# Up projection of a decoder step as a one-level Strassen product

## Chip, cores and metric

One NeuronCore of a Trainium2 chip. The metric is the device time of one execution, in microseconds (us), of the only core. TensorE is called PE below, VectorE DVE, ScalarE ACT, GpSimd POOL and the queue that issues the DMAs SP.

## The reference

One layer of a decoder, for 2048 prompt tokens and 32 sample tokens (8 sequences of 4), width 1024, in float32:

```python
h = rms_norm(x) * (1 + sc1) + sh1
proj = h @ w_in                          # two groups of heads: retention and mLSTM
x = x + g1 * (concat(y_r, y_m) @ w_out)
h2 = rms_norm(x) * (1 + sc2) + sh2
u, val = split(h2 @ w_up, [2816])        # w_up is 1024 x 5632
u = causal_conv3(u)                      # depthwise, three taps
x = x + g2 * ((silu(u) * val) @ w_down)
y = rms_norm(x) * final_w
```

The last rows of u before the convolution are outputs too. The change is in `h2 @ w_up`.

## The kernel before

Float32 accuracy is had from float16 parts. Each operand is scaled by a power of two and cut in two: a high part (ACT, a cast to float16) and a low part (DVE, value less high part). `three_passes` (L267) then adds three matmuls into one float32 bank: high by high, high by low, low by high.

The phases follow each other with a barrier between them. `phase_out` (L1573) multiplies the mixed heads by `w_out`, adds the residual, norms, and leaves `h2` transposed in SBUF, cut in its two parts (`core.h2`, features on partitions, tokens along the free axis). `phase_up` (L1918) reads it. `phase_down` (L2179) does the rest.

**phase_out** runs over 16 chunks of 128 prompt tokens and one of 32. On PE a step is the product of chunk c (48 matmuls), the transposes of the normed chunk c-1 (`turn_x`) and of the input of chunk c+2 (`turn_y`). On DVE a step is, in this order: the mean of chunk c-1, the low part of y for c+1, the scale of c+2 (a reduction and six small operations), `residual` of c (waits for the product), `h_full` of c-1 (two operations over 128x1024, `modulate`, L274) and `h_lo` of c-1, which waits for ACT's `h_hi`. ACT's order in a step is `y_hi`, `norm_x`, `scale_y`, `square`, `h_hi`. POOL does only a tiny power for each chunk (`x_rms`). The weights of the first block of `w_up` are prepared near the end of this phase.

**phase_up** runs over 22 blocks of 128 of the 2816 channels, and in a block over 5 groups of 416 tokens. For a group PE does 8 x 3 = 24 matmuls for u (bank `pu`) and 24 for val (bank `pv`). ACT copies u out (L2038), makes the first tap (L2047) and the tanh (L2056). DVE adds the two other taps (L2102), makes z (L2114), multiplies by val out of PSUM (L2118) and reduces the maximum (L2120). SP stores the result. Five groups make one block.

The next block's weights (`UpWeights`, L1870) are prepared meanwhile: SP loads them, DVE finds their maximum (L1891), POOL spreads it over the partitions (L1899, `PARTITION_ALL_REDUCE`, behind a one-element `TENSOR_TENSOR`, L1898), DVE makes the power of two (L153 to L158), ACT cuts the high part (L1903) and DVE the low part (L1907). The semaphore `lo_cut` then lets PE begin the block and SP load the block after the next. DVE also reduces the maximum of a block of `w_down` (L2143).

The order of the work on each engine is written out by hand, one queue per engine, with semaphores between them. Nothing is reordered at run time.

Of the kernel before, what the change touches and what calls it, by code (L numbers as in the profile page):

```python
# [24 lines left out]
ALU = mybir.AluOpType  # L25
# [7 lines left out]
P = 128  # L33
# [15 lines left out]
PT = [min(TG, SEQ - g * TG) for g in range(NG)]  # L49
RMS_EPS, GN_EPS = 1e-6, 1e-5  # L50
# [50 lines left out]
class Core:  # L101


    def __init__(self, nc, ctx, io):
# [9 lines left out]
        self.w_gate = self.sb(ctx, "w_gate", [P, 2, KC, P], F16)  # L114
# [36 lines left out]
def power_of_two(nc, steps, big, scale, inverse, bits):  # L151
# [188 lines left out]
def phase_ada(core):  # L340
# [3 lines left out]
    with ExitStack() as ctx:  # L344
# [96 lines left out]
        def _(dve):  # L441
# [18 lines left out]
            def factors():  # L460
# [4 lines left out]
                for s in range(2):  # L465
# [7 lines left out]
                    steps.then(last)  # L473
                nc.vector.tensor_copy(red[:, 6:8], red[:, 0:2]).then_inc(bound_here, 1)
# [1098 lines left out]
def phase_out(core):  # L1573
    nc, io = core.nc, core.io
    with ExitStack() as ctx:  # L1575
        sb, ps = (lambda *a: core.sb(ctx, *a)), (lambda *a: core.ps(ctx, *a))
        w = sb("out_w", [P, 2, KC, D], F16)
        g_p, g_s = sb("g1_p", [P, D]), sb("g1_s", [NS, D])
        y, ys = sb("o_y", [P, D]), sb("o_y_scaled", [P, D])
        sc, bits = sb("o_scales", [P, 8]), sb("o_bits", [P, 1], I32)  # L1580
        yp = sb("o_y_parts", [P, 2, 2, KC, P], F16)
        x, x1, xn = sb("o_x", [P, D]), sb("o_x1", [P, D]), sb("o_xn", [P, D])
        junk, st, half = sb("o_junk", [P, D], F16), sb("o_stats", [P, 4]), sb("o_minus_half", [P, 1])
        hf, h = sb("o_h_full", [P, KC, P]), core.h2
# [3 lines left out]
            "x_turned h_full h_hi h_lo steps half").split()}  # L1588
        part = lambda c, i, T: h[:, i, :, bass.ds(c * P, T)]
        block = ctx.enter_context(nc.Block())  # L1590
        x_rows = io["x_prompt"][0].rearrange("(c p) n -> c p n", p=P)
        xs = io["x_sample"].rearrange("b s n -> (b s) n")

        @block.sync
        def _(sp):
# [3 lines left out]
            sp.dma_start(g_p[:], core.g[0, 0:1].broadcast_to([P, D])).then_inc(s["const"], 16)  # L1599
            for u in range(DS):  # L1600
                sp.dma_start(g_s[u:NS:DS, :], core.g[0, 1:NC9]).then_inc(s["const"], 16)
# [30 lines left out]
            load_x(xs, NCH, NS)  # L1632
            save_x1(NCH, NS)
# [58 lines left out]
        def _(act):  # L1692
# [21 lines left out]
            def h_hi(c, T):  # L1714
                act.wait_ge(s["h_full"], c + 1)
                nc.scalar.copy(part(c, 0, T), hf[:, :, 0:T]).then_inc(s["h_hi"], 1)
# [8 lines left out]
            def step(c, buf, Tn):  # L1725
                y_hi(c + 1, P, 1 - buf)
# [5 lines left out]
            def pair(i):  # L1732
                step(2 * i + 1, 1, P)
                step(2 * i + 2, 0, P)

            pair(0)
            with act.Fori(1, NCH // 2 - 2) as i:
                pair(i)
            step(NCH - 3, 1, P)
            step(NCH - 2, 0, NS)  # L1740
            core.up.cut_hi(act, 0, 0)
# [3 lines left out]
            h_hi(NCH - 2, P)  # L1745
            norm_x(NCH - 1, P)
            square(NCH, NS)
            h_hi(NCH - 1, P)
            norm_x(NCH, NS)
            h_hi(NCH, NS)  # L1750

        @block.vector
        def _(dve):
# [16 lines left out]
            def residual(c, T, buf, g, steps):  # L1770
# [30 lines left out]
            dve.wait_ge(s["const"], 16 * (1 + DS))  # L1801
# [609 lines left out]
```

## Time and profile before

| | |
|---|---|
| median of 3 runs | 2946.09 us (2944.9 to 2947.54) |
| profiled execution, first to last instruction | 2944.8 us |
| PE matmuls busy | 2724.9 us, 93% |
| DVE busy | 1510.0 us, 51% |
| ACT busy | 797.8 us, 27% |
| POOL busy | 182.9 us, 6% |
| mean granted clock of PE | 0.958 of 2.4 GHz |

The profile is of one execution. PE's matmuls are pipelined: a recorded duration holds the drain, so the distance between two starts is what one costs, and a busy PE need not be a fast one. Idle time of an engine names what ended it. Idle time "until issue" is time in which the engine waited for nothing that the profile shows.

### The profile page before, as it was taken

The numbers are of one execution on the slowest core, as the hardware profiler recorded it, in microseconds if no ns is written. First come the engines' busy times: TensorE is split into PE (matmuls) and PEld (weight loads), VectorE is DVE, ScalarE is ACT, GpSimd is POOL, SyncE is SP. The second block draws the span as 40 slices with busy tenths as digits, with TensorE's granted clock in tenths as the row PEclk, the third lists the DMA queues.
The fourth block names the chain that finished last, engine by engine and source line by source line (L and its number), as shares of the span: only waits on it lengthen the run. The fifth ranks groups of instructions, "written<-read, shape, count | busy, mean of one in ns | idle before, by whom it ended". The sixth has DMA issues, their size and how long they took to land. (4 is left out here: it accounts for less than half of the span.)

```text
span 2944.8 us, 43573 instructions
## 1 busy us (share of the span) xinstructions
PE 2724.9 (93%) x16908; PEld 1547.6 (53%) x16908; DVE 1510.0 (51%) x3258; ACT 797.8 (27%) x1234; POOL 182.9 (6%) x220
## 2 busy tenths in 40 slices
PE   7898879988898999599789999999999987999998
PEld 1255445556777786355345555555555543444443
DVE  3555455544677676478645555555555545212221
ACT  1222222213444444044323222222222224111110
POOL 0022222220000000000000000000000000000000
PEclk9899899998999999699899999999999998999999
DMA  9712322143020100443122121222112217233230
GB/s 323 226 56 95 94 94 85 51 145 107 26 86 22 54 32 10 132 141 126 66 56 70 55 66 59 63 63 67 60 55 69 65 42 265 85 85 101 68 87 25
DMA packets 198730, 256.14 MB, mean 87 GB/s; under 512 B 16690, under 2 KB 146018, under 8 KB 197876
## 3 DMA queue, kind: packets, MB, share of 16 engines
q1 hardware_dynamic: 198652, 255.13, 27.7%
q8 instruction: 46, 0.75, 0.1%
q14 instruction: 32, 0.25, 0.0%
HBM read 179.88 MB, written 75.21 MB: 87 GB/s over the span
## 5 line engine op out<-in xcount | busy, mean ns | idle before, releaser
L269 PE MATMUL d_po<-d_w,d_a_parts 128*128 128x512 f16 (+1 forms) x748 | 285.5, 382 | 23.3 <-DVE d_w L2330 22.6
L269 PE MATMUL pu<-h_parts,u_w 128*128 128x416 f16 x880 | 299.1, 340 | 2.1 <-PEq L1575 2.1
L270 PE MATMUL pu<-h_parts,u_w 128*128 128x416 f16 x880 | 299.0, 340 | 0.0
L271 PE MATMUL pu<-h_parts,u_w 128*128 128x416 f16 x880 | 298.9, 340 | 0.0
L269 PE MATMUL pv<-h_parts,u_w 128*128 128x416 f16 x880 | 298.3, 339 | 0.0
L270 PE MATMUL pv<-h_parts,u_w 128*128 128x416 f16 x880 | 298.3, 339 | 0.0
L271 PE MATMUL pv<-h_parts,u_w 128*128 128x416 f16 x880 | 298.3, 339 | 0.0
L270 PE MATMUL d_po<-d_w,d_a_parts 128*128 128x512 f16 (+1 forms) x748 | 285.4, 382 | 0.0
L271 PE MATMUL d_po<-d_w,d_a_parts 128*128 128x512 f16 (+1 forms) x748 | 285.1, 381 | 0.0
L2102 DVE SCALAR_TENSOR_TENSOR u_cv<-u_in,u_conv,u_cv 128x416 f32<-128x416 f32 (+1 forms) x220 | 141.6, 644 | 199.8 <-ACT u_cv L2047 112.5
L269 PE MATMUL prj<-w_heads,h_parts_t 128*128 128x512 f16 (+1 forms) x544 | 209.2, 384 | 9.9 <-DVE h_parts_t L795 5.0
L270 PE MATMUL prj<-w_heads,h_parts_t 128*128 128x512 f16 (+1 forms) x544 | 208.8, 384 | 0.0
L271 PE MATMUL prj<-w_heads,h_parts_t 128*128 128x512 f16 (+1 forms) x544 | 208.5, 383 | 0.0
L269 PE MATMUL m_prj<-m_h,w_heads 128*128 128x128 f16 (+1 forms) x1088 | 179.5, 218 | 11.6 <-DMA m_h<-h_parts 10.3
L270 PE MATMUL m_prj<-m_h,w_heads 128*128 128x128 f16 (+1 forms) x1088 | 179.5, 218 | 0.0
L271 PE MATMUL m_prj<-m_h,w_heads 128*128 128x128 f16 (+1 forms) x1088 | 179.4, 218 | 0.0
L2317 DVE SCALAR_TENSOR_TENSOR d_out<-d_po,d_scale,g_p 128x1024 f32<-128x1024 f32 x16 | 20.5, 1283 | 287.1 <-PE d_po L271 287.1
L2038 ACT ACTIVATE u_in<-pu,u_scale 128x416 f32<-128x416 f32 (+1 forms) x110 | 65.9, 600 | 375.3 <-PE pu L271 375.3
L2056 ACT ACTIVATE u_th<-u_cv 128x416 f32<-128x416 f32 x110 | 60.4, 550 | 295.5 <-DVE u_cv L2102 258.9
L2274 ACT ACTIVATE d_a_parts<-d_a,mscale 128x2816 f16<-128x2816 f32 (+1 forms) x16 | 40.5, 2532 | 348.5 <-PE d_po L271 337.6
L269 PEld LDWEIGHTS d_po<-d_w,d_a_parts 128*128 128x128 f16 (+1 forms) x748 | 73.5, 98 | 114.9 <-issue 17.9
L269 PEld LDWEIGHTS pu<-h_parts,u_w 128*128 128x128 f16 x880 | 86.2, 98 | 70.1 <-issue 2.8
(384 smaller groups left out, 4982.0 us busy)
## 6 DMA issues: line engine op xcount, KB each, us to landing
wa<-in_w_ada_dram SPq DMA_DIRECT2D x12, 2048.0 KB, 21.7
act_cols<-u_a SPq DMA_DIRECT2D x110, 208.0 KB, 1.9
u_raw<-in_w_up_dram SPq DMA_DIRECT2D x44, 512.0 KB, 5.1
d_a<-act_cols SPq DMA_DIRECT2D x15, 1408.0 KB, 7.4
win_raw<-in_w_in_dram SPq DMA_DIRECT2D x8, 2048.0 KB, 18.5
u_wd<-in_w_down_dram SPq DMA_DIRECT2D x22, 512.0 KB, 3.6
d_raw<-in_w_down_dram SPq DMA_DIRECT2D x11, 1024.0 KB, 7.0
x_t<-in_x_prompt_dram SPq DMA_DIRECT2D x16, 512.0 KB, 4.2
```

What stands on the lines that cost most here:

```text
L269: nc.tensor.matmul(out, left[0], right[0], start=(k == 0), stop=False)
L270: nc.tensor.matmul(out, left[0], right[1], start=False, stop=False)
L271: return nc.tensor.matmul(out, left[1], right[0], start=False, stop=last)
L2038: last = nc.scalar.activation(ub[:, u, 2 + t:2 + t + n], bank[:, 0:n], ACT.Copy, scale=kv[:, u, 0:1])
L2056: nc.scalar.activation(th[:, x], cv[:, x], ACT.Tanh).then_inc(s["tanh"], 1)
L2102: ins = nc.vector.scalar_tensor_tensor(out=cv[:, x, 0:n], in0=ub[:, u, t + j:t + j + n], scalar=cw[:, u, j:j + 1], in1=cv[:, x, 0:n], op0= ...
L2274: nc.scalar.activation(ap[:, buf, 0, :, 0:T], a[:, :, 0:T], ACT.Copy, scale=core.mscale[:, 0:1]).then_inc(s["a_hi"], 1)
L2317: last = nc.vector.scalar_tensor_tensor(out=out[0:T], in0=po[0:T, buf].rearrange("p q n -> p (q n)"), scalar=ks[0:T], in1=g[0:T], op0=ALU. ...
```

## The change

The product `W^T h2` of one block is seen as a 2 x 2 block product. The rows of the left side are u and val of the block's 128 channels, the contraction is halved (4 of the 8 chunks of 128 features each), and the columns are even and odd chunks of 128 tokens. A one-level Strassen product (in Winograd's form) makes it from seven products of half the contraction, in place of eight.

- Tokens go in 3 groups of 3, 3 and 2 pairs of chunks (widths 384, 384 and 256 + 16 columns for each product). A product is 4 x 3 = 12 matmuls. A block has 3 x 7 x 12 = 252 matmuls in place of 240, over 12 x 7 x (384 + 384 + 272) = 87,360 columns in place of 99,840.
- The sums of the operands: for the weights, POOL makes four sums of 128x512 for each block (`UpWeights.sums`), ACT and DVE cut them as they cut the weights themselves (`cut_hi_sums`, `cut_lo_sums`, 128x2048), beside the weights' own parts (`cut_hi_own`, `cut_lo_own`, 128x1024 and 128x512). For the tokens, POOL makes four sums of 128x512 for each pair of chunks in `phase_out` (`h_sums`), with `sums_hi` on ACT and `sums_lo` on DVE (128x2048).
- The sums of the results are made on DVE and ACT: `keep_p1` (ACT), `keep_p16`, `odd_u` (two), `even_u`, `odd_val`, each 384 columns out of PSUM. Val of the even chunks is multiplied straight out of PSUM (`even_vz`), val of the odd ones on POOL (`odd_vz`).
- The convolution and the tanh go over 768 tokens at a time.
- The weights of `w_out` and of the up blocks share one piece of SBUF (`core.wide`), and so do the y parts and the weight sums (`core.spare`): the first block's weights are cut after the last product of `phase_out`.
- The gates `g1` of the sample tokens are loaded at the end of `phase_out` into the tile of the prompt's gates.

```diff
+UPAIRS = (3, 3, 2)
# phase_out, POOL (x_rms as before, and for each pair of chunks)
+                nc.gpsimd.tensor_tensor(t(3), b(odd, 1), b(odd, 0), ALU.subtract)
+                steps.then(nc.gpsimd.tensor_tensor(t(1), b(odd, 0), b(even, 0), ALU.subtract))
+                steps.then(nc.gpsimd.tensor_tensor(t(2), b(odd, 1), t(1), ALU.subtract))
+                nc.gpsimd.tensor_tensor(t(0), b(even, 1), t(2), ALU.subtract).then_inc(s["sums"], 1)
...
             core.up.reduce(pool, 0, 0)
-            x_rms(NCH - 2, P)
             x_rms(NCH - 1, P)
             x_rms(NCH, NS)
+            pool.wait_ge(s["prod"], NCH + 1)
+            core.up.sums(pool, 0)
+            pair_sums(NPAIR - 1)
# phase_out, ACT, one step
                 square(c, P)
-                h_hi(c - 1, P)
+                if j == 0 and not first:
+                    sums_hi(n - 1)
+                h_hi(n, j)
# phase_out, DVE, one step
+                if j == 0 and not first:
+                    sums_lo(n - 1)
+                h_full(n, j, P, steps, first)
+                h_lo(n, j)
# phase_out, DVE, the end
+            core.up.find_max(dve, 0, 0)
+            step(NPAIR - 1, 0, P, NS, 0, steps)
             core.up.find_scale(dve, 0, 0, steps)
-            step(NCH - 1, P, NS, 0, 1, steps, g_p)
+            step(NPAIR - 1, 1, NS, 0, 0, steps)
...
-            core.up.cut_lo(dve, 0, 0)
+            core.up.cut_lo_own(dve, 0, 0)
+            sums_lo(NPAIR - 1)
+            h_full(NPAIR, 0, NS, steps)
+            core.up.cut_lo_sums(dve, 0, 0)
...
# phase_up, PE: one group (product = 12 matmuls)
+            def opening(it, b, u, g, first=False):
+                if g == 0:
+                    pe.wait_ge(up.lo_cut, b + 1)
...
+                product(u, g, 1, px[:, g], True).then_inc(s["p1"], 1)
...
+                product(u, g, 6, py[:, x], True).then_inc(s["p6"], 1)
...
+                    product(u, g, 5, pz[:, x], True)
+                    pe.wait_ge(s["o1_here"], it + 1)
+                    product(u, g, 2, px[:, g], False).then_inc(s["p2"], 1)
+                    pe.wait_ge(s["o2_here"], it + 1)
...
+                    product(u, g, 7, py[:, x], False).then_inc(s["p7"], 1)
+                    if g + 1 < UG:
+                        opening(it + 1, b, u, g + 1, first)
+                    elif not last:
+                        opening(it + 1, b + 1, 1 - u, 0, first)
                     if g == 1:
                         turn_state(b)
...
+                    pe.wait_ge(s["o3_here"], it + 1)
+                    product(u, g, 4, py[:, x], False).then_inc(s["p4"], 1)
+                    pe.wait_ge(s["odd_here"], it + 1)
+                    product(u, g, 3, pz[:, x], False).then_inc(s["p3"], 1)
# phase_up, ACT: one group
+                    if not (first and g == 0):
+                        tanh(it - 1, (g - 1) % UG, first and g == 1)
...
+                        keep_p1(it + 1, b, u, g + 1, first and g == 0)
...
+                    if g == 1 and not last:
+                        up.cut_hi_sums(act, b + 1, 1 - u)
...
+                    tap0(it, b, u, g, first and g == 0)
+                    if g == 0 and not last:
...
+                        up.cut_hi_own(act, b + 1, 1 - u)
# phase_up, DVE: one group
+                    if prior:
+                        even_vz(it - 1, pu, pg)
+                    if g == 0 and not last:
+                        up.find_max(dve, b + 1, 1 - u)
+                    if g == 1 and not last:
+                        up.cut_lo_own(dve, b + 1, 1 - u)
+                        state_in(b)
...
+                    odd_u(it, u, g)
+                    if prior:
...
+                        gate(it - 1, (3 * i if back >= 0 else 3 * i - 3) + (back % 6) // 2, back % 2, pg, back % 6)
...
+                    if g == 2 and not last:
+                        block_scalars(b + 1, 1 - u)
...
+                        keep_p16(it + 1, u, g + 1)
...
+                    even_u(it, u, g)
+                    odd_val(it, u, g, first and g == 0)
+                    convolve(it, u, g, steps)
+                    if g == 0 and not last:
                         up.find_scale(dve, b + 1, 1 - u, steps)
+                    if g == 1 and not last:
+                        up.cut_lo_sums(dve, b + 1, 1 - u)
+                    if g == 2:
+                        keep_last(b, u)
...
                         nc.vector.tensor_reduce(wd_max[:, bass.ds(b, 1)], wd[:], AX.X, ALU.max, apply_absolute_value=True).then_inc(s["wd_maxed"], 1)
# phase_up, POOL: one block
+                if not last:
+                    up.reduce(pool, b + 1, 1 - u)
+                    up.sums(pool, b + 1)
+                for g in range(UG):
+                    odd_vz(UG * b + g, g, first and g == 0)
```

`gate` of a group waits for `odd_vz` of it (semaphore `vz_odd`). `state_in(b)` waits for PE's `turn_state(b)`. `up.sums` waits for the loaded weights and for the cut of the block before. The scale of the weights leaves two bits of room for the sums, the bound of the activations is multiplied by 4 (one small operation in `phase_ada`), and `w_gate` has moved to another allocation. In all other phases nothing is changed.

## Rows read from the trace of the kernel before

**Rows 1.** Busy time by stretch (us, PE, PEld, DVE, ACT, POOL, PEclk, DMA): phase_out, phase_up.

```profile
1237.00:1481.70 244.70, 215.00 (x1080) 111.12 (x1080) 167.21 (x290) 90.50 (x101) 9.82 (x19) 0.93 0.34 114
1481.70:2426.10 944.40, 938.43 (x5324) 520.08 (x5324) 500.89 (x936) 258.22 (x417) 12.13 (x43) 1.00 0.20 61
```

**Rows 2.** Timeline of PE in phase_up (start us, us), thirteen matmuls apart.

```profile
1599.80 0.34 PE L270 MATMUL pv<-h_parts,u_w 128*128 128x416 f16 x1
...
1602.09 0.34 PE L271 MATMUL pv<-h_parts,u_w 128*128 128x416 f16 x1
```

**Rows 3.** Instructions of L2143, one per block: ns min/median/max, first and last start us.

```profile
L2143 DVE TENSOR_REDUCE u_wd_max<-u_wd x22: 1208/1209/1210, 1518.6 to 2412.6; 128x1024 f32 x18, 128x1 f32<-128x1024 f32 x4
```

**Rows 4.** Groups by line and shape: busy us, mean ns of one, idle before.

```profile
L2102 DVE SCALAR_TENSOR_TENSOR u_cv<-u_in,u_conv,u_cv 128x416 f32<-128x416 f32 x176 | 114.4, 650 | 115.7 <-ACT u_cv L2047 112.5 <-issue 0.2
...
L2114 DVE SCALAR_TENSOR_TENSOR u_z<-u_th,u_cv 128x416 f32<-128x416 f32 x110 | 65.2, 593 | 67.8 <-ACT u_th L2056 67.8
L2047 ACT ACTIVATE u_cv<-u_in,u_conv 128x416 f32<-128x416 f32 x88 | 64.5, 733 | 8.1
L2120 DVE TENSOR_REDUCE u_max<-u_a 128x1 f32<-128x416 f32 x110 | 64.5, 586 | 3.8
...
L1907 DVE SCALAR_TENSOR_TENSOR u_w<-u_raw,u_red,u_w 128x2048 f16<-128x2048 f32 x22 | 51.7, 2348 | 0.0
...
L1891 DVE TENSOR_REDUCE u_red<-u_raw 128x1 f32<-128x2048 f32 x22 | 50.1, 2276 | 0.0
...
L1903 ACT ACTIVATE u_w<-u_raw,u_red 128x2048 f16<-128x2048 f32 x22 | 43.7, 1987 | 11.3 <-DVE u_scale L1894 11.3
...
L1778 DVE SCALAR_TENSOR_TENSOR o_x<-po,o_scales,g_p 128x512 f32<-128x512 f32 x32 | 22.5, 746 | 18.3 <-PE po L271 13.7 <-ACT o_xn L1707 4.7
```

**Rows 5.** Timeline of POOL around two all-reduces (phase_out; weights of mLSTM).

```profile
1439.67 0.18 POOL L1898 TENSOR_TENSOR u_carrier<-u_carrier 1x1 f32<-1x1 f32 x1 [13.99 <-DVE u_red L1891]
1445.69 0.38 POOL L1899 PARTITION_ALL_REDUCE u_red<-u_red  x1 [5.83 <-issue]
1452.97 0.59 POOL L1856 TENSOR_TENSOR o_stats<-o_stats,o_minus_half 128x1 f32<-128x1 f32 x1 [6.91 <-issue]
...
238.26 1.25 POOL L928 TENSOR_TENSOR rot_sin<-qk_raw_t,rope_t 128x512 f32<-128x512 f32 x1 [7.01 <-issue]
```

**Rows 6.** Timeline of DVE and POOL where operations with two SBUF inputs meet.

```profile
258.95 4.48 DVE L263 SCALAR_TENSOR_TENSOR mlsw_cut<-win_raw,mlsw_red,mlsw_cut 128x4096 f16<-128x4096 f32 x1
...
261.31 3.24 POOL L928 TENSOR_TENSOR rot_sin<-qk_raw_t,rope_t 128x512 f32<-128x512 f32 x1 [3.07 <-ACT qk_raw_t L732]
264.51 2.25 POOL L929 TENSOR_TENSOR rot_sin<-qk_raw_t,rope_t 128x512 f32<-128x512 f32 x1
```

**Rows 7.** Busy time by stretch (columns as in rows 1): a gap of PE, and after it.

```profile
1245.00:1249.00 4.00, 0.01 (x1) 0.00 (x0) 2.37 (x8) 1.15 (x1) 0.00 (x0) 1.00 0.00 0
1249.00:1252.00 3.00, 2.99 (x12) 2.09 (x13) 0.00 (x0) 0.00 (x0) 0.00 (x0) 0.53 0.47 175
```

**Rows 8.** Timeline of phase_out: one chunk's distance, ACT's square, the stall and the end.

```profile
1376.20 0.15 DVE L1785 TENSOR_SCALAR o_stats<-o_stats 128x1 f32<-128x1 f32 x1
...
1383.21 1.06 ACT L1712 ACTIVATE o_junk<-o_x 128x1024 f16<-128x1024 f32 x1 [2.24 <-DVE o_x L1780]
...
1388.53 0.15 DVE L1785 TENSOR_SCALAR o_stats<-o_stats 128x1 f32<-128x1 f32 x1
...
1454.80 1.97 PE L1663 MATMUL o_tpx<-identity,o_xn 128*128 128x128 f32 x8 [13.35 <-ACT o_xn L1707]
...
1468.44 0.38 PE L269 MATMUL po<-out_w,o_y_parts 128*32 128x512 f16 x1
...
1481.01 0.43 DVE L1794 TENSOR_TENSOR h_parts<-o_h_full,h_parts 128x256 f16<-128x256 f32 x1 [0.47 <-ACT h_parts L1716]
```

**Rows 9.** Timeline of SP at the start of phase_out: the sample gates.

```profile
1235.23 2.71 SPq L1601 DMA_DIRECT2D g_s<-gates_ada  x4
```

**Rows 10.** Timeline of POOL at the end of phase_up.

```profile
2422.76 0.37 POOL L2176 PARTITION_ALL_REDUCE u_max<-u_max  x1 [69.42 <-DVE u_max L2165]
```

More of the change, by code:

```diff
@@ L49 @@
 PT = [min(TG, SEQ - g * TG) for g in range(NG)]
+NPAIR = NCH // 2
+HALF_T = NT // 2
+UPAIRS = (3, 3, 2)
+UG = len(UPAIRS)
+UT = [2 * P * sum(UPAIRS[:g]) for g in range(UG + 1)]
+UDEC = [0, 0, NS // 2]
 RMS_EPS, GN_EPS = 1e-6, 1e-5
@@ L1587, in phase_out @@
             "const w_in0 w_in1 y_in x_in y_scale y_scaled y_turned y_hi y_lo prod x1_here x1_saved x_sq x_mean x_rms xn_ready "
-            "x_turned h_full h_hi h_lo steps half").split()}
-        part = lambda c, i, T: h[:, i, :, bass.ds(c * P, T)]
+            "x_turned h_full h_hi h_lo sums sum_steps sums_hi sums_lo steps half dec_gate").split()}
+        flat = lambda a: a.rearrange("p m k t -> p (m k) t")
+        half_k = KC // 2
         block = ctx.enter_context(nc.Block())
@@ L1851, in _ @@
+            core.up.cut_lo_sums(dve, 0, 0)
+            dve.wait_ge(s["h_hi"], NCH + 1)
+            for to, of in dec:
+                last = nc.vector.tensor_tensor(to(1), of, to(0), ALU.subtract)
+            last.then_inc(s["h_lo"], 1)
+            sums_lo(NPAIR)
         @block.gpsimd
@@ new lines, in own, with of_sums, cut_hi_own @@
+    def own(self, u, i):
+        return ((self.w[:, u, i, 0:2].rearrange("p m k n -> p (m k) n"), self.raw[:, :, 1, :]), (self.w[:, u, i, 2], self.raw[:, KC // 2:KC, 0, :]))
+    def of_sums(self, u, i):
+        return self.w[:, u, i, 3:7].rearrange("p m k n -> p (m k) n"), self.wsum.rearrange("p m k n -> p (m k) n")
+    def cut_hi_own(self, act, b, u):
+        act.wait_ge(self.scaled, b + 1)
+        for to, of in self.own(u, 0):
+            last = self.nc.scalar.activation(to, of, ACT.Copy, scale=self.red[:, u, 2:3])
+        last.then_inc(self.hi_own, 1)
@@ new lines, in cut_hi_sums, with lo_of, cut_lo_own @@
+    def cut_hi_sums(self, act, b, u):
+        act.wait_ge(self.scaled, b + 1)
+        act.wait_ge(self.summed, b + 1)
+        to, of = self.of_sums(u, 0)
+        self.nc.scalar.activation(to, of, ACT.Copy, scale=self.red[:, u, 2:3]).then_inc(self.hi_sums, 1)
+    def lo_of(self, u, lo, of, hi):
+        return self.nc.vector.scalar_tensor_tensor(out=lo, in0=of, scalar=self.red[:, u, 2:3], in1=hi, op0=ALU.mult, op1=ALU.subtract)
+    def cut_lo_own(self, dve, b, u):
+        dve.wait_ge(self.hi_own, b + 1)
+        for (lo, of), (hi, _) in zip(self.own(u, 1), self.own(u, 0)):
+            self.lo_of(u, lo, of, hi)
@@ L2083, in _ @@
             body(FB - 2, 0)
-            body(FB - 1, 1, prep=False)
+            body(FB - 1, 1, last=True)
+            tanh(N_IT - 1, UG - 1)
             copy_last(FB - 1)
@@ new lines, in even_u, with odd_val @@
+            def even_u(it, u, g):
+                x = par(u, g)
+                dve.wait_ge(s["p4"], it + 1)
+                last = scaled_add(of_half(ub[:, 2 + UT[g]:2 + SEQ], g, 0), by_pair(py[:, x], g), u, by_pair(o1[:, x], g))
+                if UDEC[g]:
+                    last = scaled_add(new_s(0), seqs(rest(py[:, x], g)), u, seqs(rest(o1[:, x], g)))
+                last.then_inc(s["even_here"], 1)
+            def odd_val(it, u, g, early=False):
+                x, n = par(u, g), width(g)
+                dve.wait_ge(s["p3"], it + 1)
+                if not early:
+                    dve.wait_ge(s["vz_odd"], it)
+                scaled_add(ov[:, 0:n], pz[:, x, 0:n], u, o2[:, x, 0:n]).then_inc(s["val_here"], 1)
```

492 lines of the change are left out of this document (310 added, 182 removed).

## The prediction

> **What bounds the kernel now.** I read the stages first. phase_up takes 944.4 us and PE is busy in 938.4 of them, at the full clock; phase_out takes 245 us with PE busy in 215 and DVE in 167 [rows 1]. Then the distance of two matmuls: 13 starts of 416 columns in 2.29 us, 0.176 us each, which is 416 columns at 2.4 GHz and 2.9 ns [rows 2]. 240 of them make 42.3 us, and a block takes (2412.6 - 1518.6)/21 = 42.57 us [rows 3]. So phase_up is PE without a gap, and DVE works 501 of 944 us. In phase_out a chunk of 128 tokens takes 1388.53 - 1376.20 = 12.33 us [rows 8]; 48 matmuls of 512 columns and 16 transposes fill it, but DVE waits for a product only 18.3/16, about 1 us, per chunk [rows 4]. That phase has little room on DVE. Last, POOL: after an all-reduce its next ordinary operation starts only 6.9 to 7.0 us later, with nothing to wait for, and from an ordinary operation to an all-reduce 6.0 us pass [rows 5]. At the end of phase_up, where an all-reduce follows an all-reduce, nothing of this is seen [rows 10]. I read it as a switch in each direction. Before, POOL has nothing else to do in a block, and both switches cost nothing.
>
> **PE's part.** A matmul of 384 columns costs 160 + 2.9 = 163 ns, one of 272 costs 116 ns. A block: 168 x 0.163 + 84 x 0.116 + 0.2 for two transposes = 37.3 us. One stall is built in: DVE's `state_in` stands before `odd_u` in group 1, and waits for a transpose that PE does only after the opening of group 2, while product 4, next on PE, waits for `odd_u`'s first sum. Copy 0.17, sum 0.62, hops: 1.0 us. So 38.4 us a block if all else is covered, 4.2 us less than now, 92 us in 22 blocks. What decides is whether it is covered.
>
> **DVE's and ACT's operations** grow by 1.04 ns (DVE: 650 ns at 416 columns, 2348 at 2048) and 0.85 ns (ACT) for each column [rows 4]. So 384 columns out of PSUM cost 0.62, 272 columns 0.50, a tap over 768 tokens 1.02, the gate 0.96, its maximum 0.95, first tap on ACT 1.03. DVE's sum for a block is some 34 us, under 38.4. It would fit if the work came evenly.
>
> **The ring that sets the block.** The weights of the next block go around once per block, through queues in a fixed order:
> 1. POOL, from the end of `find_max`: 6.0 to the all-reduce, 0.4, 6.9 back [rows 5], then four sums of 128x512 at 1.25 and 0.2 of hops = 5.2, held up 0.7 by DVE's cut with two SBUF inputs (`cut_lo_own`), then `odd_vz` of group 0, 0.95 (by elements; at most the 1.25 of 512). 20.2 us. `odd_vz` needs only the convolution, but stands behind reduce and sums in POOL's queue.
> 2. DVE has waited in `gate` for `vz_odd`. Queued behind that wait: gate 0.96, maximum 0.95, `keep_p16` 0.50, `even_u` 0.62, then ACT's first tap 1.03, two taps 2.03, `cut_lo_sums` 2.35. Less overlaps, 8.3 us. `lo_cut` comes only now; PE has stood before product 1 of the next block for some 3.7 us.
> 3. PE: restart 0.1, products 1 and 6 (3.9), 4 and 3 of group 2 (2.8), drain 0.2. 7.0 us.
> 4. DVE: `odd_val` 0.5, two taps 2.0, copies 0.3, maximum of w_down 1.2, `even_vz` 0.7, `find_max` 2.3, less overlaps: 6.4 us, and the ring is closed.
>
> Sum 41.9 us. I add 0.3 for waits still to be passed after the one that came last. And the gap of PE: after one of 4.0 us its granted clock was 0.53 over the next 3 us, half of 2.4 GHz [rows 7]; 3 us at half the clock is about 1.6 us of lost work, in leg 3. A gap of 3.7 us may or may not do this; bounds 0 and 1.6, I take half, 0.8. The block: 43.1 us, against 42.57. PE's gain is eaten by its own stall.
>
> phase_up: 21 x 43.1 = 905.1; the last block has no next one, 38.4; half clock at the start 1.6; behind the last product the rest of the chain on DVE and ACT 6.3; the end 9.9, of which 3.9 as before and 6.0 for the final all-reduce, which now follows an ordinary operation [rows 5, 10]. 961 us, against 944.4: +17.
>
> At one point a rule bears on leg 1. The trace has 6.9 us for the way back to ordinary operations [rows 5]. The Trainium skill (GPSIMD Engine Reference, "Instruction dispatch") says that the first call of a freshly loaded kernel pays a code load of about 6 us; it names the way in, not the way out. By that rule alone leg 1 would be 13.3 us and the sum that of the first rival below, 2930 us. I go by the rows.
>
> **phase_out, the loop.** For every pair of chunks POOL makes four sums (5.1 us, in the shade), ACT casts 128x2048 (2.0) and DVE cuts 2.35 [rows 4]. But `sums_hi` stands on ACT behind `square` (1.06 + 0.19, [rows 8]), which starts only when DVE's residual is done, and DVE comes to `sums_lo` 0.5 us after that: it waits 1.25 + 2.0 - 0.5 = 2.75 us, then works 2.35. Behind it on DVE stand `h_full`, `h_lo`, and the scale of the input that PE's next transposes need. 5.1 us less a slack of about 0.8 (most of that 1 us of waiting) leaves 4.3 us a pair, 26 us for six pairs. One thing is gained: PE's stall of 13.35 us near the end [rows 8], where DVE stood waiting for the all-reduce, is 12.5 us shorter since `find_scale` comes a step after `find_max`. Net +13.5.
>
> **phase_out, the end.** From PE's last product (start 1468.44) to the last cut (1481.44) 12.5 us pass [rows 8]. After: POOL is back from the all-reduce 4.7 us behind the last product and norm, residual and `h_full` of chunk 15 follow up to 14.4; then on POOL four weight sums and four token sums, 10.2 with 1.3 of waiting for DVE: 25.8; cast 2.0, cut 2.35: 30.1; `h_full` of the sample tokens, `cut_lo_sums`, the small cuts: 35.5 us. +23. The four sample-gate DMAs leave the start of the phase, 2.7 us of issue ahead of the second load of y [rows 9]: -3. At the end of the phase they lie beside a product of some 10 us, nothing. Moved allocations, two bits of scale and one operation in phase_ada: nothing over 0.2 us.
>
> Sum: 2944.8 + 17 + 13.5 + 23 - 3 = 2995; the profiled execution stands 1.3 us under the median, so **2997 us**, 1.7% slower.
>
> **Rivals.**
> - *The way back of POOL is free or overlaps* (faster). It decides where leg 1 falls below some 17 us; DVE then no longer waits for `vz_odd`, PE's wait for `lo_cut` falls to about 1 to 2 us, and a block takes 39.3 to 40.5. With 39.9: 21 x (43.1 - 39.9) = 67 us less, 2930 us. Against it: 6.91 and 7.01 us before two different operations [rows 5]. For it: both were seen once the all-reduce was done, and part of the way back could lie beside something else here.
> - *Everything is covered*: 38.4 a block, 99 us less than forecast, 2898 us. It needs the first rival and no wait for `lo_cut` at all, though convolution and `cut_lo_sums` (4.4 us) follow product 3, and PE reaches that wait 4.2 us after it.
> - *POOL and DVE block each other* (slower still). A POOL operation of 1.25 us took 3.24 us under a DVE operation with two SBUF inputs, the next 2.25 [rows 6]. I have 0.7 us of it in leg 1. If each sum takes 2.2, leg 1 grows by 4 and the last phase of sums too; with half of that and the clock lost in each block: 45 us a block, 3037 us; with all of it 3075.
> - That seven products aren't what runs has no room: the count of columns is fixed by the code.
>
> **How the numbers follow.** Forecast 0.68, free way back 0.12, all covered 0.05, mutual blocking 0.15. The range holds the forecast with its clock bounds (2980 to 3015), the first rival and the middle of the third: 2925 to 3040. A measurement of this kernel can tell about 0.2% (6 us) from no change. Faster 0.16, same 0.03, slower 0.81.
>
> **What would show it.** Right: the distance of two L2143-like reductions near 43 us; POOL idle "until issue" near 6.9 before the first weight sum; DVE's gate of group 0 waiting some 3 us for POOL; PE waiting 3 to 4 us once a block for the cut of the sums, and 1 us for the first odd sum; DVE waiting near 2.75 us for ACT's cast of the sums in phase_out, pairs of chunks 29 us apart. Wrong: PE dense through phase_up; sums that start right behind the all-reduce; a first block's weights that are ready when phase_out's last product ends.

## The result and the profile after

The changed kernel takes **3031.8 us** (median of four runs, 3024.2 to 3036.5) against 2946.8 of the kernel before in the same session: 1.0286 times as long, interval 1.0269 to 1.0303. The forecast was 2997 us, 1.7% slower.

First, where the 85 us are. The table gives, for the profiled execution of each kernel, the time from phase_out's first maximum of y to phase_up's first matmul, and from there to phase_down's first matmul; block is the steady distance from one block to the next.

| kernel | phase_out starts | phase_out | phase_up | block |
|---|---|---|---|---|
| before | 1229.1 | 252.7 | 956.4 | 42.6 |
| changed | 1235.5 | 300.6 (+48.0) | 993.2 (+36.8) | 44.4 |

The start of phase_out (6 us later here) isn't the change's: the nine experiments below, which leave everything ahead of it alike, start it between 1225.1 and 1233.4. The code ahead of it is the same but for one small operation.

**The ring.** Timeline of POOL in the changed kernel over one block; it answers to [rows 5].

```profile
1988.08 0.18 POOL L1981 TENSOR_TENSOR u_carrier<-u_carrier 1x1 f32<-1x1 f32 x1 [3.08 <-DVE u_red L1977]
1994.09 0.38 POOL L1982 PARTITION_ALL_REDUCE u_red<-u_red  x1 [5.83 <-issue]
2002.16 1.26 POOL L1998 TENSOR_TENSOR spare_parts<-u_raw 128x512 f32<-128x512 f32 x1 [7.69 <-issue]
2003.39 1.70 POOL L1999 TENSOR_TENSOR spare_parts<-u_raw 128x512 f32<-128x512 f32 x1
...
2007.73 1.00 POOL L2440 TENSOR_TENSOR u_vz<-u_val,u_cv 128x384 f32<-128x384 f32 x1
```

And of DVE, behind it:

```profile
2000.99 2.97 DVE L2023 SCALAR_TENSOR_TENSOR wide_weights<-u_raw,u_red,wide_weights 128x1024 f16<-128x1024 f32 x2 [1.30 <-ACT wide_weights L2013]
...
2009.06 0.96 DVE L2354 SCALAR_TENSOR_TENSOR u_a<-u_th,u_vz 128x768 f32<-128x768 f32 x1 [3.60 <-POOL u_vz L2440]
...
2015.07 2.35 DVE L2023 SCALAR_TENSOR_TENSOR wide_weights<-spare_parts,u_red,wide_weights 128x2048 f16<-128x2048 f32 x1
...
2026.08 0.50 DVE L2289 SCALAR_TENSOR_TENSOR u_val<-pz,u_scale,u_p 128x272 f32<-128x272 f32 x1 [0.76 <-PE pz L2154]
...
2030.14 2.27 DVE L1977 TENSOR_REDUCE u_red<-u_raw 128x1 f32<-128x2048 f32 x1
```

The only two waits of PE over 0.1 us in the same block, and then its clock (columns as in [rows 1]) ahead of, right behind and well after the longer one:

```profile
2004.86 0.34 PE L2152 MATMUL py<-h_parts,wide_weights 128*128 128x384 f16 x1 [0.80 <-DVE u_p L2289]
2017.47 0.50 PE L2152 MATMUL px<-h_parts,wide_weights 128*128 128x384 f16 x1 [4.37 <-DVE wide_weights L2023]
```

```profile
2005.00:2013.00 8.00, 8.00 (x60) 5.67 (x58) 3.83 (x6) 2.98 (x2) 3.58 (x4) 1.00 0.13 49
2017.40:2020.40 3.00, 2.92 (x10) 1.41 (x11) 2.93 (x7) 0.00 (x0) 0.88 (x1) 0.50 0.00 0
2026.00:2040.00 14.00, 14.00 (x88) 8.42 (x86) 10.30 (x18) 2.79 (x5) 1.47 (x4) 1.00 0.21 61
```

Read in a circle: find_max ends at 1988.0; POOL changes over to the all-reduce, back, makes four sums and the gate product, and lets DVE's gate start at 2009.06 (**21.06 us**); DVE and ACT come to the cut of the sums, which ends at 2017.42 (**8.36**) and starts PE; PE works at half clock, 1.2 instead of 2.4 GHz, then at full, until DVE takes product 3 of the last group at 2026.08 (**8.66**, hops included); the next find_max ends at 2032.41 (**6.33**). The sum, 44.4, is the distance of the find_maxes: 44.3 to 44.8 in 19 of the 20 distances inside phase_up.

The way back of 7.69 us in this block is a long one: over the kernel's 22 all-reduces of the up weights it is 6.63 to 7.80, median 6.98. The block hardly varies with it, because the first sum runs beside DVE's cut: it starts 13.2 to 14.2 us behind find_max's end and ends 15.4 to 15.5 behind it, in 18 of 21 blocks. A block's four sums take 6.2 us here and 5.0 in e2, where they miss the cut: DVE and POOL cost each other 1.2 us.

**phase_out.** Timelines of DVE, ACT and PE over one pair of chunks; the pair takes 1409.32 - 1378.20 = 31.1 us, where [rows 8] have 2 x 12.33. The mean of six pairs is 31.4, and 24.5 in the kernel before.

```profile
1378.20 0.15 DVE L1824 TENSOR_SCALAR o_stats<-o_stats 128x1 f32<-128x1 f32 x1
...
1389.21 0.15 DVE L1824 TENSOR_SCALAR o_stats<-o_stats 128x1 f32<-128x1 f32 x1
...
1402.14 2.29 DVE L1842 TENSOR_TENSOR h_parts<-o_h_sums,h_parts 128x2048 f32 x1 [2.96 <-ACT h_parts L1745]
...
1409.32 0.14 DVE L1824 TENSOR_SCALAR o_stats<-o_stats 128x1 f32<-128x1 f32 x1
```

```profile
1398.87 1.06 ACT L1734 ACTIVATE o_junk<-o_x 128x1024 f16<-128x1024 f32 x1 [4.79 <-DVE o_x L1819]
...
1399.92 1.88 ACT L1745 CAST h_parts<-o_h_sums 128x2048 f32 x1
```

```profile
1380.29 1.97 PE L1685 MATMUL o_tpx<-identity,o_xn 128*128 128x128 f32 x8 [3.43 <-ACT o_xn L1729]
1383.03 1.97 PE L1664 MATMUL tpy<-identity,o_y_scaled 128*128 128x128 f32 x8 [0.77 <-ACT o_y_scaled L1724]
```

ACT casts the sums behind its square, DVE waits 2.96 us for that and then works 2.29. What follows from it is in the PE rows: PE stands 3.43 us, and both groups of eight transposes take 1.97 us; undisturbed they take 1.04 and 1.09. The granted clock was 0.50 meanwhile:

```profile
1380.20:1385.80 5.60, 4.74 (x19) 3.73 (x20) 4.87 (x13) 2.14 (x3) 0.00 (x0) 0.50 0.28 91
```

### The profile page after: what moved, and what is told of

Same layout as the page of the kernel before. It is cut to its first block and busy times, and to the rows that moved or that the text cites. A ratio compares the mean times of both kernels' runs of the same rounds, so it can differ in the third digit from the quotient of the medians.

```text
span 3034.7 us, 44808 instructions
## 1 busy us (share of the span) xinstructions
PE 2668.0 (88%) x17172; PEld 1594.7 (53%) x17172; DVE 1701.4 (56%) x3489; ACT 792.3 (26%) x1134; POOL 467.4 (15%) x432
## 5 line engine op out<-in xcount | busy, mean ns | idle before, releaser
L2152 PE MATMUL px<-h_parts,wide_weights 128*128 128x384 f16 (+1 forms) x528 | 179.8, 341 | 106.1 <-DVE wide_weights L2023 87.0
L2152 PE MATMUL py<-h_parts,wide_weights 128*128 128x384 f16 (+1 forms) x792 | 246.2, 311 | 18.9 <-DVE u_p L2289 18.8
L2153 PE MATMUL py<-h_parts,wide_weights 128*128 128x384 f16 (+1 forms) x792 | 245.8, 310 | 0.0
L2154 PE MATMUL py<-h_parts,wide_weights 128*128 128x384 f16 (+1 forms) x792 | 245.8, 310 | 0.0
L2153 PE MATMUL px<-h_parts,wide_weights 128*128 128x384 f16 (+1 forms) x528 | 178.4, 338 | 0.0
L2154 PE MATMUL px<-h_parts,wide_weights 128*128 128x384 f16 (+1 forms) x528 | 176.6, 335 | 0.0
L2152 PE MATMUL pz<-h_parts,wide_weights 128*128 128x384 f16 (+1 forms) x528 | 163.9, 310 | 0.0
L2153 PE MATMUL pz<-h_parts,wide_weights 128*128 128x384 f16 (+1 forms) x528 | 163.9, 310 | 0.0
L2154 PE MATMUL pz<-h_parts,wide_weights 128*128 128x384 f16 (+1 forms) x528 | 163.9, 310 | 0.0
L2440 POOL TENSOR_TENSOR u_vz<-u_val,u_cv 128x384 f32<-128x384 f32 (+1 forms) x66 | 103.0, 1561 | 381.8 <-DVE u_cv L2332 220.7
L2329 DVE SCALAR_TENSOR_TENSOR u_cv<-u_in,u_conv,u_cv 128x768 f32<-128x768 f32 x132 | 122.5, 928 | 16.1 <-ACT u_cv L2231 13.1
```

Source lines behind the costliest of these rows:

```text
L2152: nc.tensor.matmul(out, left[0], right[0], start=(start and k == 0), stop=False, skip_group_check=True)
L2153: nc.tensor.matmul(out, left[0], right[1], start=False, stop=False, skip_group_check=True)
L2154: last = nc.tensor.matmul(out, left[1], right[0], start=False, stop=(k == KC // 2 - 1), skip_group_check=True)
L2329: ins = nc.vector.scalar_tensor_tensor(out=cv[:, 0:n], in0=ub[:, t:t + n], scalar=cw[:, u, j:j + 1], in1=cv[:, 0:n], op0=ALU.mult, op1=ALU ...
L2440: last = nc.gpsimd.tensor_tensor(of_half(vz, g, 1), by_pair(ov, g), of_half(cv, g, 1), ALU.mult)
```

## The experiments

Each is a small edit of the changed kernel. "Block" is the mean distance of the reduction of w_down (the line of [rows 3]), total the median, the ratio is to the kernel before.

| kernel | phase_out | phase_up | block | total | ratio, interval |
|---|---|---|---|---|---|
| changed | 300.6 | 993.2 | 44.0 | 3031.8 | 1.0286, 1.0269 to 1.0303 |
| e1_no_switch | 299.2 | 889.7 | 39.1 | 2928.8 | one run |
| e2_two_switches | 313.3 | 1276.2 | 56.8 | 3324.0 | one run |
| e3_pe_filler | 300.7 | 960.4 | 42.5 | 3000.7 | 1.0177, 1.0159 to 1.0194 |
| e4_sums_first | 300.7 | 890.4 | 39.2 | 2930.5 | 0.9943, 0.9923 to 0.9964 |
| e5_out_late | 271.8 | 992.1 | 44.0 | 2997.6 | 1.0183, 1.0158 to 1.0208 |
| e6_first_turn | 302.4 | 887.6 | 39.0 | 2925.4 | 0.9941, 0.9920 to 0.9962 |
| e7_first_turn_late | 273.7 | 897.4 | 39.5 | 2902.4 | 0.9844, 0.9815 to 0.9872 |
| e8_dma_turn_late | 265.2 | 915.2 | 40.4 | 2917.9 | 0.9903, 0.9882 to 0.9924 |
| e9_gap_turn_late | 272.0 | 893.3 | 39.2 | 2897.4 | 0.9840, 0.9823 to 0.9856 |

The means hold the last, shorter distance (34.9 to 35.8, the block that prepares no next one); the steady distance of the changed kernel is 44.4, that of e1 and e4 39.2 and that of e3 42.7 to 43.1. phase_out, phase_up and block are of one profiled execution, the total is the median of all.

**No change-over of POOL.**

```diff
-        self.nc.gpsimd.partition_all_reduce(self.red[:, u, 1:2], self.red[:, u, 0:1], P, MAX_OVER_PARTITIONS).then_inc(...)
+        self.nc.gpsimd.tensor_tensor(self.red[:, u, 1:2], self.red[:, u, 0:1], self.red[:, u, 0:1], ALU.add).then_inc(...)
```

> The maximum over the partitions is left out: the all-reduce of each block becomes an ordinary 128x1 addition, so POOL changes over neither to nor from it in the up phase; the sums, the cuts and the products stay. Theory (the block is set by the ring find_max, POOL's two changes, sums, gate, convolution, cut, product): 13 us leave a ring of 44.4, the next limit is PE and DVE work at 39 to 40 us a block; phase_up about 868 instead of 981, the end of phase_out some 10 shorter, total about 2910. Rival (DVE work with the more expensive weight cuts, or PE at its lower clock, is the bound and the ring only lies beside it): over 43 us a block, total over 3000. Rival (DVE and GpSimd block each other while both read two operands): the sums and the cuts are all still there, so no more than 1 us a block comes off, total over 3005.

The kernel leaves out the maximum over the partitions. 39.2 us a block, 5.2 less; phase_up lost 103.5 us, with every sum, cut and product in place (phase_up and total still lie 22 and 19 us above this run's own forecast). So DVE's work doesn't hold the block at 44, and mutual blocking is a small part: the four sums take 5.5 us a block, 0.7 less. PE's wait for the cut is down to 16.5 us in 21 blocks, and behind phase_up's first 3 us no stretch at half clock is left in its blocks. In medians, the leg from find_max to the gate is 17.4 us for 21.0 and leg 3 is 7.06 for 8.69; the other two stay. POOL has its gate product 11.0 us behind find_max here, so the 17.4 are DVE's own queue. The end of phase_out hardly moved (phase_out -1.5, forecast 10).

**Two change-overs more.**

```diff
+        self.nc.gpsimd.partition_all_reduce(self.spread[:, u:u + 1], self.red[:, u, 0:1], P, MAX_OVER_PARTITIONS)
+        self.nc.gpsimd.tensor_tensor(self.carrier2[:], self.carrier2[:], self.carrier2[:], ALU.add)
         self.nc.gpsimd.partition_all_reduce(self.red[:, u, 1:2], self.red[:, u, 0:1], P, MAX_OVER_PARTITIONS).then_inc(...)
```

> Each block does its all-reduce twice, with an ordinary 1x1 addition between: one more way back to ordinary operations and one more way in. Theory: all of it lies on the ring, 6.9 + 5.9 + 0.4 = 13.2 us a block in 21 blocks, about +277, total about 3310. Rival (the ring isn't what sets the block): less than half of it comes through, below +7 a block, total under 3180.

+292 us, and steady blocks of 57.6 to 58.5 in one profiled execution. Timeline of POOL:

```profile
2017.96 0.38 POOL L1984 PARTITION_ALL_REDUCE u_spread<-u_red  x1 [5.80 <-issue]
2025.01 0.18 POOL L1985 TENSOR_TENSOR u_carrier<-u_carrier 1x1 f32<-1x1 f32 x1 [6.67 <-issue]
2030.95 0.38 POOL L1986 PARTITION_ALL_REDUCE u_red<-u_red  x1 [5.75 <-issue]
2038.98 1.25 POOL L2002 TENSOR_TENSOR spare_parts<-u_raw 128x512 f32<-128x512 f32 x1 [7.65 <-issue]
```

A pair of change-overs costs 2030.95 - 2017.96 = 13.0 us in this block, the least of 22 (median 13.4, up to 14.2), and it comes through: the median block is 13.5 us longer. 12.5 of these lie between find_max and the gate, the pair less the 1.2 us that the sums no longer lose to the cut, and 1.0 in leg 3, where PE's clock was at half for longer. Each direction is paid each time, before a 1x1 and a 128x512 operation alike (6.7 to 7.7 and 6.6 to 7.7). The way in, 5.7 to 6.3 us, agrees with the about 6 us that the Trainium skill (GPSIMD Engine Reference, "Instruction dispatch") gives for the first call of a freshly loaded kernel; the way back is the trace's alone.

**PE kept busy through the wait.**

```diff
+                if g == 0 and not first:
+                    for _ in range(2):
+                        product(1 - u, 0, 1, px[:, 0], True)
+                    pe.wait_ge(up.lo_cut, b + 1)
```

> In the 4.4 us in which PE waits at a block's start for the cut of the summed weights it repeats a finished product twice (24 matmuls of 384 columns, 3.9 us, thrown away). Theory of the half clock (the first 3 us of work after the gap run at half clock because PE had stood idle, and this costs the ring 1.6 us a block): 44.4 becomes 42.8, phase_up about -34, total about 2998. Rival (the slow matmuls are made up for elsewhere in the block, or the clock falls for another reason): 44.4 stays, total within 5 of 3032. If the filler itself comes late and delays the product: above 3032.

-31 us, 42.8 for 44.4: as the theory had it. No stretch at half clock is left in the ring, and leg 3 takes 7.06 us for 8.69. Behind the filler the first 3 us of product 1 run at the full clock:

```profile
1996.90:1999.90 3.00, 2.98 (x19) 1.81 (x20) 2.93 (x6) 0.00 (x0) 0.83 (x1) 1.00 0.00 0
```

So the half clock costs the ring 1.6 us, the full difference and not half of it, and thrown-away work was the cheaper way to wait here.

**The order of two calls.**

```diff
                 if not last:
-                    up.reduce(pool, b + 1, 1 - u)
                     up.sums(pool, b + 1)
+                    up.reduce(pool, b + 1, 1 - u)
```

> The only edit is the order of two calls on GpSimd in the up phase: a block's four weight sums stand ahead of its all-reduce instead of behind it. Same work, same two changes. Theory: POOL idles 3.1 us ahead of find_max's end, the sums of 5.2 us start there, so that 3 to 5 us leave the ring of 44.4: 39.3 to 41.4 us a block, phase_up 870 to 915, total 2925 to 2970. Rival (what counts is the work of POOL, DVE and their blocking, not the order): 44 us a block, total 3025 to 3040. Rival (all of POOL's leg is one chain, and the sums ahead only delay the scale as much as they shorten the rest): 44.4 minus less than 1.

-101 us by an edit that removes no work: now faster than the kernel before. Timeline of POOL:

```profile
2086.86 1.28 POOL L1998 TENSOR_TENSOR spare_parts<-u_raw 128x512 f32<-128x512 f32 x1
...
2092.02 0.67 POOL L1981 TENSOR_TENSOR u_carrier<-u_carrier 1x1 f32<-1x1 f32 x1
2098.55 0.46 POOL L1982 PARTITION_ALL_REDUCE u_red<-u_red  x1 [5.86 <-DVE u_val L2289]
```

The sums start while POOL would have waited for find_max (ended at 2089.9) and hold the all-reduce up by 2.1 us only. Of their 5.2 us, 3.1 leave the ring, and they no longer lie beside the cut (5.1 us for 6.2). The gate now starts 17.4 us behind find_max instead of 21.0, no later than in e1, where POOL changes over not at all. That is 3.6 of the 5.2 us that the block fell by; the other 1.6 are the clock, which the shorter gap of PE gave back: no stretch at half clock is left in the ring. The whole of phase_up (columns as in [rows 1]), and then the same of the changed kernel:

```profile
1527.00:2405.60 878.60, 830.13 (x5588) 544.25 (x5588) 670.24 (x1154) 237.53 (x305) 235.17 (x215) 0.99 0.21 66
```

```profile
1536.18:2517.30 981.12, 863.00 (x5588) 554.82 (x5588) 674.49 (x1154) 239.91 (x305) 246.02 (x215) 0.96 0.19 59
```

33 of the 103 us are PE's own busy time; DVE works 670 and 674 us.

**phase_out's token sums cut one chunk later.**

```diff
# ACT
-                square(c, P)
-                if j == 0 and not first:
+                if j == 1 and not first:
                     sums_hi(n - 1)
+                square(c, P)
...
# DVE
-                if j == 0 and not first:
+                if j == 1 and not first:
                     sums_lo(n - 1)
```

> Only phase_out's loop is edited: a pair's token sums are cut one chunk later, the cast (ACT) ahead of the odd chunk's square and the difference (DVE) behind the odd chunk's residual, where the cast has long ended. Theory (of the 6.4 us that a pair takes more, 31.1 instead of 24.7, 2.7 are DVE's wait for the cast, and 2 are PE's half clock after the gap that this wait opens; the 2.3 of the difference itself stay): 31.1 becomes 26 to 27, six pairs, phase_out 304 becomes 275 to 280, total 3002 to 3008. Rival (the sums on GpSimd hold back the normalisation, and that sets the pair): the pair stays above 30, total within 5 of 3032.

At the end of the loop ACT's last cast moves in the same way. Pairs of 26.3 us (12.4 and 13.9) for 31.1, phase_out 28.8 shorter, total -34: a little more than expected. Of the 4.8 us of the pair 2.96 are DVE's wait; the other 1.8 fit the clock, for in the loop no stretch at half clock is left. ACT's cast now lies at 1383.06, ahead of the square, and DVE's wait is gone, its 2.29 us stay:

```profile
1386.03 2.29 DVE L1842 TENSOR_TENSOR h_parts<-o_h_sums,h_parts 128x2048 f32 x1 [0.26 <-DVE o_scales L1807]
```

```profile
1371.00 1.09 PE L1664 MATMUL tpy<-identity,o_y_scaled 128*128 128x128 f32 x8 [1.74 <-ACT o_y_scaled L1724]
```

**State rows turned right behind product 7**, on top of the new order of sums.

```diff
                     product(u, g, 7, py[:, x], False).then_inc(s["p7"], 1)
+                    if g == 1:
+                        turn_state(b)
...
-                    if g == 1:
-                        turn_state(b)
```

> On top of the kernel with the sums ahead of the all-reduce (39.2 us a block) the transposition of the state rows is moved from behind the next group's opening to right behind product 7, so that DVE can take it in four us earlier. Theory (39.2 is 37.3 of products and the 1.0 us that PE waits each block for DVE behind that transposition, and some waits of 0.9): 38.2 to 38.6 a block, total 2910 to 2918. Rival (DVE's work of the block is the limit, so the wait moves): 39.2 stays, total within 4 of 2930.

A miss: 2925.4 against 2930.5, ratios of 0.9941 and 0.9943, 39.0 against 39.2 a block. The theory's wait went, and came back elsewhere. Waits of PE from 1560 to 2380 (us in total, times, longest), first without, then with the edit:

```profile
PE px L2152 <- DVE wide_weights L2023: 18.7, 21, 1.9
PE py L2152 <- DVE u_p L2289: 15.9, 20, 0.8
```

```profile
PE px L2152 <- DVE wide_weights L2023: 32.2, 21, 2.5
```

The rival (the wait moves) was right in effect: 15.9 us fewer at one wait, 13.5 more at the other. POOL's change-overs were still on the ring (DVE's gate waits for the gate product there), so earlier work of DVE only waited longer: the gate starts 17.35 us behind find_max, as before the edit.

**All three edits of order together**, those of e4, e5 and e6.

> All three edits of order together: sums ahead of the all-reduce, state rows turned early, token sums of phase_out cut a chunk late. Theory: they lie in different stages and add up: 2930 less 12 to 20 less 24 to 30, 2882 to 2894 in all, faster than the kernel before (2947 to 2949) by some 2%. If they do not add up: above 2900.

2902.4 us, 1.6% faster than the kernel before, but short of the theory's 2882 to 2894 (one of four executions, 2890.8, lies in it; the profiled one, 2906.6, is the slowest): phase_up lies 7 to 10 us above e4 and e6. Behind the first distance, which is long in e1, e4 and e6 too (42.0 to 42.6), five of the other 19 are 41.3 to 41.9 us instead of some 39. In one PE waits 2.23 us for the cut; in another, 39 long, 1.28:

```profile
1779.74 0.34 PE L2152 MATMUL px<-h_parts,wide_weights 128*128 128x384 f16 x1 [2.23 <-DVE wide_weights L2023]
...
2097.89 0.34 PE L2152 MATMUL px<-h_parts,wide_weights 128*128 128x384 f16 x1 [1.28 <-DVE wide_weights L2023]
```

```profile
1780.00:1792.48 12.48, 12.48 (x76) 7.74 (x75) 8.47 (x21) 2.61 (x5) 2.18 (x4) 0.86 0.39 117
...
2095.00:2104.90 9.90, 8.62 (x65) 6.06 (x64) 7.61 (x14) 2.37 (x4) 3.05 (x1) 1.00 0.31 99
```

The clock fell in the one block and not in the other. These are exactly the five blocks with a stretch of 3.4 us at half clock; e4 has none of them and e6 one, in its one block of 41.4. Five times the 1.6 us of e3 are 8 us, what phase_up lies above e4 and e6. The gap alone doesn't tell which block it hits: here it followed gaps of 2.02, 2.12, 2.23, 2.40 and 2.63 us and not others of 2.09, 2.12 and 2.22. Why some blocks get the longer gap isn't shown.

**The maximum through DRAM**, in place of POOL's all-reduce; the state rows and the token sums are moved as in e7, the weight sums stand where the change put them.

```diff
+    def spread_max(self, sp, b, u):
+        sp.wait_ge(self.maxed, b + 1)
+        sp.dma_start(self.max_row[u], self.red[:, u, 0:1]).then_inc(self.max_out, 16)
+        sp.wait_ge(self.max_out, 16 * b + 16)
+        sp.dma_start(self.all_max[:, u, :], self.max_row[u:u + 1, :, 0].broadcast_to([P, P])).then_inc(self.max_in, 16)
```

> The maximum over partitions without GpSimd's library call: the 128 maxima go to DRAM and come back to every partition as a row in two transfers of SP's queue (4 to 5 us by the 1.9 to 2.7 us that small transfers take here), and DVE reduces the row; GpSimd does ordinary operations alone until the end of the up phase, the weight sums stand as in the changed kernel. With the state rows and the token sums moved as in the run before. Theory: nothing of POOL's changes is left on any path; the block is 38.2 to 38.6 as there, and the end of phase_out is 6 to 10 us shorter, since the normalisation no longer waits 6.9 us behind the all-reduce: 2872 to 2888. Rival (the two transfers are slower or stand behind the saves of SP's queue): the scale comes over 13 us after the maximum and the block is 40 or more, total over 2920.

Half right: phase_out is 8.4 us shorter than e7's (forecast 6 to 10), but the blocks take 40.4, and 2917.9 us lie above the forecast's 2888. The issues of DMAs (KB each, median us from issue to landing) show the term that was mis-sized:

```profile
u_all_max<-up_max_row SPq DMA_DIRECT2D x22, 64.0 KB, 4.6
up_max_row<-u_red SPq DMA_DIRECT2D x22, 0.5 KB, 7.2
```

11.8 us instead of 4 to 5, close to the 13 of the rival. Waits from 1560 to 2380, of DVE for the row and of PE for DVE's first odd sum, which stands behind it in DVE's queue:

```profile
DVE u_red L1989 <- DMA u_all_max<-up_max_row: 36.6, 20, 2.4
PE py L2157 <- DVE u_p L2294: 33.6, 20, 2.2
```

1.8 us a block, and PE passes on 1.7 of them. Five blocks have a stretch at half clock here too. How much of the 7.2 comes from the 128 pieces of four bytes and how much from the 512 KB of w_down that the same queue issued 2.6 us earlier wasn't tried.

**Weight sums where POOL waits anyway**, with the other two edits of e7.

```diff
                 for g in range(UG):
+                    if g == 2 and ahead:
+                        up.sums(pool, b + 2)
                     odd_vz(UG * b + g, g, first and g == 0)
...
+                    up.load_raw(sp, b + 2)
                 save_a(b, 1, par(u, 1))
```

> The kernel with all three edits of order (39.1 us a block), with a block's weight sums moved once more: from behind the last gate product of the block before (where they still push the all-reduce 2.1 us behind find_max) to ahead of it, into the stretch in which POOL waits 8.6 us for DVE's convolution; the weights' transfer is issued ahead of the second save of activations so that it is there in time. Theory (in the run with the state rows turned early PE's one wait was that for the cut, 1.5 us a block, because the ring was the limit again): 2.1 us leave the ring, PE's wait goes, 37.8 to 38.5 a block, 13 to 25 off 2902: total 2877 to 2890. Rival (DVE's work, 32 us of 39, with its small waits for PE is the limit now): the block stays at 39, total 2895 to 2905. Rival (the sums now lie beside DVE's convolutions and gates, which read two operands too, and slow them, or the weights come too late and delay the gate product): over 39.5, total over 2910.

2897.4 us, no gain over e7 that the runs can tell; the block stays at 39.2 (39.5 in e7), and PE still waits 1.6 us a block for the cut. By its numbers the first rival holds, by its cause the second. The same stretch in both kernels, e7 first:

```profile
1530.00:2360.00 830.00, 794.25 (x5309) 518.52 (x5308) 638.41 (x1091) 225.91 (x290) 226.58 (x204) 0.99 0.21 66
```

```profile
1530.00:2360.00 830.00, 795.60 (x5346) 519.74 (x5345) 674.05 (x1094) 226.75 (x291) 225.56 (x204) 1.00 0.21 66
```

DVE's busy time rises from 638 to 674 us for the same work, 1.7 us a block: the sums of 1.3 us now lie beside its convolutions, which read two operands from SBUF, and the two hold each other up as in [rows 6]. In medians the leg from find_max to the gate is down from 17.35 us (e6) to 14.82, and the last leg, from product 3 to the end of find_max, is up from 6.34 to 9.04, so the ring gains nothing. One sum of POOL and one tap of DVE beside the sums, 0.75 us long elsewhere:

```profile
2094.26 1.28 POOL L1998 TENSOR_TENSOR spare_parts<-u_raw 128x512 f32<-128x512 f32 x1 [5.03 <-DMA u_raw<-in_w_up_dram]
```

```profile
2098.52 1.81 DVE L2330 SCALAR_TENSOR_TENSOR u_cv<-u_in,u_conv,u_cv 128x512 f32<-128x512 f32 x1
```

The sums lie there because the weights come late: POOL waits 5.0 us for the transfer, 101 us in 20 blocks. What the edit would bring with the weights there in time wasn't tried.

## Why the prediction was right, and where its sizes were off

The direction, the mechanism and the range hold: PE's 12% less work (42.3 to 37.3 us a block) is bought with a ring through POOL, and that ring, not work, sets the block. e1, e2 and e4 show it from three sides. The size was too small: 51 us forecast, 85 measured. Of the difference 20 us lie in phase_up and 15 in phase_out, and most of both is the half clock of PE.

- **PE's part.** 37.3 us of products and transposes: e4 has 830.13 / 22 = 37.7. The built-in stall of 1.0 is 0.80 a block. Right. That a block could fall to 38.4 if all is covered was too good: no kernel here got below a mean of 39.0.
- **Leg 1, 20.2 forecast, 21.06 measured (median 21.0).** In the block shown the way back took 7.69 us against 6.9, and sums and gate product 6.9 us from the first sum to the gate's start against 5.2 + 0.7 + 0.95. In the median block it is the other way round: the way back is 7.0 us, and from the first sum to the gate 7.5 pass. So the missing 0.8 are mostly a hold-up by `cut_lo_own` of 1.2 us where I had 0.7; one sum took 1.70 while that cut was still running.
- **Legs 2 and 4**, 8.3 and 6.4: 8.36 and 6.33.
- **Leg 3, 7.0 + 0.8 forecast, 8.66 measured.** This is the step that failed, in size: the gap of PE was 4.4, not 3.7, and I took half the price of the clock. Without half clock the leg takes 7.06 (e3, e4), and the full 1.6 applies. The terms of my block, 41.9 + 0.3 + 0.8, make 43.0, not 43.1. With the other half of the clock and leg 1's 0.85 they make 44.65, less the 0.3 of waits that I had added and that aren't there: 44.4.
- **phase_up** forecast +17, measured +36.8: 21 x 0.9 (mean distance 44.0 for 43.1) = 19.
- **The end of phase_up.** The final all-reduce starts 6.23 us after the last gate product, as forecast with 6.0. DVE had its last maximum at 2511.8, so 3.4 us of them were left to wait for:

```profile
2508.67 0.23 POOL L2442 TENSOR_TENSOR u_vz<-u_val,u_cv 128x16 f32<-128x16 f32 x1
2515.13 0.37 POOL L2460 PARTITION_ALL_REDUCE u_max<-u_max  x1 [6.23 <-issue]
```

- **phase_out's loop**, 29 a pair forecast, 31.1 measured. The wait for the cast (2.75, now 2.96) and the work (2.35, now 2.29) are right. Left out was what this does to PE's clock: the wait opens a gap of 3.4 us in PE in each pair, and the half clock behind it costs about 2 us. Six pairs, 12 of the 15 us missed in this phase. I had the row for it [rows 7] and used it in phase_up alone. The slack of 0.8 rests on a row that I read too broadly: of the 18.3 us only 13.7 are DVE's wait for a product [rows 4], 0.9 a chunk.
- **phase_out's end**, 35.5 forecast: from the end of the last product at 1501.9 to PE's start at 1536.2, 34.3 us. Right. The wait of the normalisation behind the all-reduce is there too, though taking it away alone made phase_out 1.5 us shorter (e1), and 8.4 where the token sums had moved (e8 against e7); which wait ended last there isn't settled:

```profile
1497.52 1.31 POOL L1982 PARTITION_ALL_REDUCE u_red<-u_red  x1 [5.80 <-issue]
1505.77 0.59 POOL L1916 TENSOR_TENSOR o_stats<-o_stats,o_minus_half 128x1 f32<-128x1 f32 x1 [6.94 <-issue]
```

- **The start of phase_out**, -3 forecast: not told apart from the spread of the phases ahead.
- **Rivals.** The free way back (2930): excluded by 6.67 and 7.65 us in e2. So is what the Trainium skill's rule alone would have made of leg 1: 2930 forecast, 3032 measured. All covered (38.4 a block): never as a mean, even without any change-over. Mutual blocking: there, 1.2 us in leg 1 where I had 0.7 and this rival 2 to 4. Its forecast of 45 a block and 3037 us lies close to the result for a wrong reason, since most of the missing microseconds were the clock's; and its own terms, 2 and the clock's 0.8 on top of 43.1, make 45.9.
- **A slope.** By [rows 4] ACT's operations grow by (1987 - 733)/(2048 - 416) = 0.77 ns a column, not 0.85. The first tap would be 1.00 us for 1.03: nothing that moves the sum.

## What to carry to other kernels

Before work goes to an engine with an order of its own, write down the circle that a block's data makes through all queues, with every change of library in both directions, and put what depends on nothing (here four sums) ahead of the slow step instead of behind it: that swap alone was worth 3.3% and turned the change from 2.9% slower to 0.6% faster. A gap of PE of 3 us and more was priced twice, by its length and by the half clock behind it, in both stages in which it opened; shorter gaps were so only at times. When a wait is removed, look at the next one at once: two of the edits here only moved it.

## What was not expected of the hardware

- Behind a gap of PE of 3.1 to 4.4 us at a block's start the clock was 0.50 for some 3.4 us, each time (the changed kernel and e5). Behind gaps of 1.98 to 2.85 it did so 13 times in e6 to e9 and not 7 times, the longest of those 2.47. Behind shorter ones (up to 1.88) it never did, in any kernel but e2, whose gaps follow each other too closely to tell.
- An all-reduce costs 5.7 to 6.5 us on the way in and 6.6 to 7.8 on the way back, every time, 13.0 to 14.2 us for a pair with only a 1x1 operation between.
- 0.5 KB in pieces of four bytes took 7.2 us to DRAM, right behind a transfer of 512 KB in the same queue; the 64 KB that came back took 4.6.
- POOL's gate product of 384 columns took 3.04 us where it met DVE's cut of the sums, and 1.00 elsewhere.
- The first sum's start varied by 1.0 us with the way back, and its end by 0.1, where DVE's cut ran beside it: a hold-up can hide the spread of a slow step from the block's time.
